# Decay and rate low-rank products in two row halves of the array, with their biases from fp32r products

## The reference

```
r, k, v, wd, ad, gd = split(h)                       # wd, ad: 64 wide
w_log = -softplus(-(w0 + tanh(wd) @ w_lora_up)) - 0.5
decay = exp(-exp(w_log))
a     = sigmoid(a0 + ad @ a_lora_up)                 # both 512 wide
```

## Time and profile before

| what | value |
|---|---|
| median of 3 runs | 2969.92 us (2968.96 to 2973.3) |
| the profiled execution | span 2963.8 us from the first to the last instruction, no other time is given for it; 6.1 us below the median |
| TensorE busy | 2899.2 us, 98% |
| VectorE, ScalarE, GpSimd busy | 54%, 34%, 50% |
| mixer | from about 597 to 1045 us of the span |

### The profile page before, as it was taken

One profiled execution on the slowest core, in us unless ns is written; L12 is line 12 of the kernel. 1 busy time (PEld: TensorE's weight loads), 2 busy tenths in 40 slices (PEclk: granted clock), 3 DMA queues, 4 the chain that ended last, 5 costly groups with the idle time before them and its releaser, 6 DMA issues. The chain is left out here.

```text
span 2963.8 us, 56296 instructions
## 1 busy us (share of the span) xinstructions
PE 2899.2 (98%) x23690; PEld 2474.9 (84%) x23690; DVE 1594.7 (54%) x2059; ACT 1000.5 (34%) x1740; POOL 1489.8 (50%) x1073
## 2 busy tenths in 40 slices
PE   8999999999999999999999999999999999999998
PEld 7888888888888879987888888887998788888887
DVE  7331634267777732329766654544233966664453
ACT  4122211245545432325333332232232533332222
POOL 4554544356666545266554533555427555543254
PEclk9999999989999999999999999999999999999999
DMA  4533455412223231112333356344111233336632
GB/s 160 183 114 96 126 167 183 146 50 61 65 57 80 71 100 43 43 50 76 115 119 140 128 192 223 142 175 156 42 46 49 85 114 135 138 111 238 230 142 85
DMA packets 175988, 346.65 MB, mean 117 GB/s; under 512 B 47233, under 2 KB 104705, under 8 KB 170113
## 3 DMA queue, kind: packets, MB, share of 16 engines
q1 hardware_dynamic: 175744, 343.16, 34.0%
HBM read 240.34 MB, written 102.76 MB: 116 GB/s over the span
## 5 line engine op out<-in xcount | busy, mean ns | idle before, releaser
L820 POOL TENSOR_TENSOR w_lo<-w_raw,w_hi 128x512 fp32r<-128x512 f32 x232 | 333.6, 1462 | 504.5 <-ACT w_hi L1124 501.0
L1679 PE MATMUL ps<-a_hi,w_hi 128*128 128x512 f32 x1140 | 445.3, 391 | 10.4 <-DVE a_lo L2396 10.0
L1679 PE MATMUL ps<-a_lo,w_hi 128*128 128x512 f32 x1140 | 444.3, 390 | 0.0
L1679 PE MATMUL ps<-a_hi,w_lo 128*128 128x512 f32 x1140 | 351.5, 390 | 0.0
L1124 ACT ACTIVATE w_hi<-w_raw 128x512 fp32r<-128x512 f32 x228 | 129.9, 623 | 625.5 <-PE ps L1679 474.7
L2216 PE MATMUL ps<-a_hi,w_hi 128*128 128x512 f32 x800 | 312.4, 391 | 11.5 <-ACT u_t L1499 4.9
L2216 PE MATMUL ps<-a_lo,w_hi 128*128 128x512 f32 x800 | 311.3, 389 | 0.0
L2216 PE MATMUL ps<-a_hi,w_lo 128*128 128x512 f32 x800 | 311.3, 389 | 0.0
L1679 PEld LDWEIGHTS ps<-a_hi,w_hi 128*128 128x128 f32 x1140 | 214.5, 188 | 55.0 <-DVE a_lo L2396 10.0
L1679 PEld LDWEIGHTS ps<-a_hi,w_lo 128*128 128x128 f32 x1140 | 214.3, 188 | 44.8
L1679 PEld LDWEIGHTS ps<-a_lo,w_hi 128*128 128x128 f32 x1140 | 214.5, 188 | 44.2 <-issue 0.2
(11 more groups left out here) (379 smaller groups left out, 6429.3 us busy)
## 6 DMA issues: line engine op xcount, KB each, us to landing
w_raw<-in_weights SPq DMA_DIRECT2D x228, 512.0 KB, 4.1
hidden<-hid SPq DMA_DIRECT2D x44, 1024.0 KB, 3.8
zT<-z_out SPq DMA_DIRECT2D x44, 512.0 KB, 3.3
a_hi<-hidden SPq DMA_DIRECT2D x44, 512.0 KB, 8.3
a_lo<-hidden SPq DMA_DIRECT2D x44, 512.0 KB, 9.4
w_raw<-kvw SPq DMA_DIRECT2D x32, 512.0 KB, 3.3
suv<-zT SPq DMA_DIRECT2D x16, 512.0 KB, 4.7
x<-in_xT SPq DMA_DIRECT2D x16, 512.0 KB, 6.0
```

The costliest lines, as they stand in the source:

```text
L820: pool.tensor_tensor(low_t[:, part, :], w_raw[:, u, part, :], high[:, part, :].bitcast(F32), ALU.subtract).then_inc(S["w_lo_done"], 1)
L1679: mm = pe.matmul(to[:, nb, 0:w], wt[:, k, :], r[:, k, nb * w:(nb + 1) * w], start=(k == 0 and r is hi_in and wt is high), stop=(k == kn - ...
```

## The change

The decay's and the rate's low-rank values come in one tile wad, decay in rows 0 to 63 and rate in rows 64 to 127, with two transfers in place of four. The weights lie in one tile wal in the same way. The products of the two halves alternate. The biases no longer have a row of ones. Two fp32r products of 32 rows each write them into the whole of bank 4 and bank 5 first: lora_b holds the biases by 128-channel block (a high and a remaining part in separate rows), ind is 1 where a row belongs to the block of 128 columns. VectorE prepares lora_b and ind in spatial().

```diff
-ZK_DMAS, ZV_DMAS = 10, 5
+ZK_DMAS, ZV_DMAS = 8, 5
...
-        wl = rw("wl", [P, RH * RN])
-        al = rw("al", [P, RH * RN])
+        wal = rw("wal", [P, RH * RN])
+        ind = rw("ind", [RN, HP * L], F32R)
+        lora_b = rw("lora_b", [RN, P], F32R)
...
-                for dst, src in ((wl, w_lora), (al, a_lora), (gl, g_lora), ...
+                for dst, src in ((wal, lora_up), (ind_in, lora_ind), (bias_in, lora_bias), (bias_sel, lora_sel), (gl, g_lora), ...
...
-                both_ways(wd[par][0:RN], zT[24], n, f"zk{par}")
-                both_ways(ad[par][0:RN], zT[25], n, f"zk{par}")
+                both_ways(wad[par], zT_t[12], n, f"zk{par}")
...
-            for t in (wd[0], ad[0], wd[1], ad[1]):
-                pool.memset(t[RN:P, :], 1.0).then_inc(S["rconst_done"], 1)
-            pool.wait_ge(S["rconst_done"], N_ONES)
...
-                act.activation(wd[par][0:RN, :], wd[par][0:RN, :], ACT.Tanh).then_inc(S["lora_in"], 1)
+                act.activation(wad[par][0:RN, :], wad[par][0:RN, :], ACT.Tanh).then_inc(S["lora_in"], 1)
...
-                low_rank(wl, wd[par], 4)
-                low_rank(al, ad[par], 5).then_inc(S["lwa_ps"], 1)
+                for e in range(2):
+                    rows = slice(32 * e, 32 * e + 32)
+                    pe.matmul(ps[:, 4 + e, :], lora_b[rows, :], ind[rows, :], start=True, stop=False, skip_group_check=True)
+                for m in range(HP):
+                    for e in range(2):
+                        mm = pe.matmul(cols(4 + e, m), wal[lane(e), m * P:(m + 1) * P], wad[par][lane(e), (m // 2) * C:(m // 2) * C + L],
+                                       start=False, stop=True, skip_group_check=True)
+                mm.then_inc(S["lwa_ps"], 1)
...
-                dve.wait_ge(S["rconst"], 16 * 19)
+                dve.wait_ge(S["rconst"], 16 * 21)
...
                 dve.wait_ge(S["const_ready"], 7)
+                dve.tensor_copy(ind[:], ind_in[:]).then_inc(S["rconst_done"], 1)
+                dve.tensor_copy(lora_b[:], bias_in[:]).then_inc(S["rconst_done"], 1)
+                dve.wait_ge(S["rconst_done"], 2)
+                dve.tensor_scalar(bias_in[:], bias_in[:], bias_sel[:, 0:1], None, ALU.mult).then_inc(S["rconst_done"], 1)
+                dve.wait_ge(S["rconst_done"], N_BIAS - 1)
+                dve.scalar_tensor_tensor(lora_b[:], lora_b[:].bitcast(F32), bias_sel[:, 1:2], bias_in[:], ALU.mult, ALU.add
+                                         ).then_inc(S["rconst_done"], 1)
+                dve.wait_ge(S["rconst_done"], N_BIAS)
                 dve.tensor_scalar(hc[:, 0, :], hc[:, 0, :], 0.5, None, ALU.mult).then_inc(S["const_ready"], 1)
```

More of the change, by code:

```diff
@@ L29 @@
 HP = RH // 2
-N_ONES, N_SET = 4, 6
+N_BIAS, N_SET = 4, 6
 L = 128
@@ L69, with hybrid_block_kernel @@
 G_IN, G_ATT, G_FF, G_FINAL, G_MEM = range(5)
[L72 removed]
+def hybrid_block_kernel(nc, xT, memT, gains, weights, shift_mu, lora_up, lora_bias, lora_sel, lora_ind, g_lora, head_cols,
                         kk_rows, lnx_rows, kk_cols, head_ones, w_spatialT, b_spatial, sgu_ln, consts, cen,
@@ L199, in hybrid_block_kernel @@
         wsr = place("wsr", [P, RH, L], F32, Z_END + 5 * KB)
-        wl = rw("wl", [P, RH * RN])
-        al = rw("al", [P, RH * RN])
+        ind_in = place("ind_in", [RN, HP * L], F32, Z_END + 9 * KB)
+        bias_in = place("bias_in", [RN, P], F32, Z_END + 15 * KB)
+        bias_sel = place("bias_sel", [RN, 2], F32, Z_END + 15 * KB + 512)
+        wal = rw("wal", [P, RH * RN])
+        ind = rw("ind", [RN, HP * L], F32R)
+        lora_b = rw("lora_b", [RN, P], F32R)
         gl = rw("gl", [P, RH * RN])
@@ L226, in hybrid_block_kernel @@
         suv = [rw(f"suv{i}", [P, 8, L]) for i in range(2)]
-        wd = [rw(f"wd{i}", [P, 3 * C]) for i in range(2)]
-        ad = [rw(f"ad{i}", [P, 3 * C]) for i in range(2)]
+        wad = [rw(f"wad{i}", [P, 3 * C]) for i in range(2)]
         gd = [rw(f"gd{i}", [P, 3 * C]) for i in range(2)]
@@ L548, in load_consts @@
                 sp.wait_ge(S["kvf_lo"], 2)
-                for dst, src in ((wl, w_lora), (al, a_lora), (gl, g_lora), (hc, head_cols), (kkr, kk_rows), (lnr, lnx_rows),
+                for dst, src in ((wal, lora_up), (ind_in, lora_ind), (bias_in, lora_bias), (bias_sel, lora_sel), (gl, g_lora), (hc, head_cols), (kkr, kk_rows), (lnr, lnx_rows),
                                  (heads, head_ones), (kkc, kk_cols), (hm, head_mean), (cent, cen), (id_in, half_ident), (tri_w, tri_wide),
@@ L3200 @@
     arrays["shift_mu"] = A(col(shift_mu[0]))
-    def padded(*parts):
-        parts = np.concatenate([np.asarray(r) for r in parts], 0)
-        out = np.zeros((P,) + parts.shape[1:], np.float32)
-        out[:parts.shape[0]] = parts
-        return out
-    arrays["w_lora"] = padded(w_lora_up[0], w0[0][None])
-    arrays["a_lora"] = padded(a_lora_up[0], a0[0][None])
+    arrays["lora_up"] = A(np.concatenate([np.asarray(w_lora_up[0]), np.asarray(a_lora_up[0])], 0))
+    bias = np.zeros((2, 32, P), np.float32)
+    sel = np.zeros((2, 32, 2), np.float32)
+    ind = np.zeros((2, 32, HP, L), np.float32)
+    for e, b in enumerate((w0, a0)):
+        for m in range(HP):
+            for r in (m, HP + m):
+                bias[e, r] = np.asarray(b[0]).reshape(HP, P)[m]
+                ind[e, r, m] = 1.0
+            sel[e, m] = 0.0, 1.0
+            sel[e, HP + m] = 1.0, -1.0
+    arrays["lora_bias"], arrays["lora_sel"], arrays["lora_ind"] = bias.reshape(RN, P), sel.reshape(RN, 2), ind.reshape(RN, HP * L)
     arrays["g_lora"] = A(np.asarray(g_lora_up[0]))
```

## The result

The changed kernel takes 2977.06 us (median of 20 runs, 2970.41 to 2982.95) against 2969.61 for the kernel before (20 runs, one of them stray at 14473): a ratio of 1.0026, 95% interval 1.0019 to 1.0032. It is slower by 7.5 us, where 2.8 faster was forecast, and outside the range. The two profiled executions differ by as much: spans of 2971.4 and 2963.8, so this pair of traces holds a loss of the same size.

What follows compares the result with a forecast made beforehand. TensorE, busy 98% of the span, was taken as the bound. The mixer's -5.6 us and the entry's +2.8 summed to -2.8, so 2969.9 became 2967.1 us, with a range of 2961 to 2973.

Steps and rivals of the forecast that it cites:

- rival 3: At the entry, the 4.75 us stall lowers TensorE's clock to half; short form 2968.8, long form 2978.1 at 0.08.
- the long form: At the entry, the 11.0 us job behind the stall runs at half clock: +11.0, total 2978.1 us; chance 0.08.
- the short form: At the entry, 3.4 us at half clock cost 1.7 us, total 2968.8; counted as upper part of the 0.42 forecast.
- The saving per group: In the mixer, decay and rate products fall from 1.88 to 1.53 us per group, saving 0.35; ends 0.00 and 0.55.
- the change of shape behind the keys' turn: In each mixer group, going from whole array to 32-row strips ahead of the bias products costs 0.10 us.
- beside each other, 0.23: In each mixer group, the two 32-row bias products run together in 0.23 us, not in turn at 0.46.
- Rival 2: In the mixer, array drains at each shape change and bias products run in turn: no saving, 2972.7 us; chance 0.13.
- The entry: Preparation in spatial(): TensorE starts its next job 4.75 us later, less 1.08, 0.45 and 0.4 given back: +2.8 us.
- Rival 1: At the entry, new VectorE instructions slip through together: 2963.6 us, chance 0.22; halfway, two of them free: 2965.2, chance 0.15.
- VectorE's turns with GpSimd: At the entry, four new VectorE instructions and hc each get in between two GpSimd instructions, hc done at 548.05.
- the two waits of 1.08 and 0.45: TensorE's waits before the first loras and on the suv transfer vanish, giving back 1.08 and 0.45 us.
- The saving in the mixer reaches the end: The group's later work shifts along, no new wait; 14 groups give 4.9 us and group 1 0.7, together 5.6.

Runs made afterwards that it cites:

- e1: Changed kernel with VectorE's four bias instructions moved two pairs earlier; 2974.79 us, +4.0 against the kernel before.
- e4: Kernel before plus only the new transfers and four VectorE bias instructions, result unused; 2975.91 us, +5.1 against the kernel before.
- e2: Changed kernel with group 1's 16 products as whole-array instructions; 2971.80 us, +1.0 against the kernel before.
- e3: Changed kernel with the bias instructions early and group 1's 16 products on the whole array; 2967.41 us, -3.4 against the kernel before.
- e7: e5 with bias products of 64 rows, 32 of them zeros; 2958.22 us, -11.3 against the kernel before.
- e13: Changed kernel with bias products of 64 rows, 32 of them zeros, preparation left in place; 2971.91 us, +2.1 against the kernel before.
- e9: e1 with group 1's 16 half-row products issued once more, ahead of the bias pair; 2967.02 us, ratio 0.9998 against the kernel before.
- e5: e1 with five redundant whole-array products filling TensorE's two longest pauses of body(-1); 2961.06 us, -8.5 against the kernel before, in two clumps.
- e8: e5 without the bias products, so the output lacks w0 and a0; 2951.56 us, -18.0 against the kernel before.
- e10: e1 with group 1's 16 half-row products reordered, eight of one half then eight of the other; 2974.95 us, +4.4 against the kernel before.

## Why the prediction was wrong

**The step that failed** is the clock in rival 3. It looked for the price of a low clock only where the change makes a new pause, at the entry, and gave the long form 0.08 there. At that place the dip was short (3.4 us at half, 1.7 lost), as the short form had it. The long half clock came at a place where the change makes no pause, where the clock was already at half, and where the products that the change replaces were the ones behind which it came back. The prediction read those rows for their length (group 1 saves 0.7) and not for the clock's return beside them. The sum had no term for it, and it cost 7.1 us net of the shorter products. That the cause is group 1's products and not the entry is shown by e1 (no entry pause, long half clock), e4 (entry pause, no long half clock) and e2 and e3 (whole-array products again, no long half clock, with and without the entry pause). That the time landed near the 2978.1 of the long form is luck: that form held the job behind the entry's pause at half clock for 11.0 us, which didn't happen.

**Terms that were mis-sized.**
- The saving per group: forecast 0.35, measured 0.27. The 16 products (1.10, measured 1.09) and the change of shape behind the keys' turn were right. The term that failed is the bias products "beside each other, 0.23" with 0.10 for the change behind: the pair takes 0.42 to 0.44 in all, with 64 rows it takes 0.23 (e7). The two do start beside each other, within 0.02 us; the time goes ahead of the next shape. Rival 2's full drain (no saving) did not occur.
- The entry: forecast +2.8 net of a stall of 4.75, measured +3.9. TensorE's pause was 4.04 us. The dip of the clock is 1.7 of the 3.9; without it the entry would be at 2.2. e1 minus after is -3.5 when each is taken against its own kernel before, so the runs agree. Rival 1, the quick entry, did not occur. Its sum is off by a little in itself: it finds 1.2 us for the five instructions and goes on with 1.3, and 1.3 - 1.08 - 0.45 - 0.4 is -0.6, not -0.7.

**Steps that were right.** VectorE's turns with GpSimd, one for one, with hc at 547.68 (forecast 547.9); no cover for the folded copy; the two waits of 1.08 and 0.45 at the first loras gone. The saving in the mixer reaches the end: from_values to from_values is 27.5 us on average after (639.49 to 969.60, twelve groups) and 27.75 before (628.21 to 961.21, twelve), 0.24 a group.

**What stays open.** It is shown that whole-array products for group 1 bring the clock back. Why 16 half-row products do so in some traces and not in others is open. A 32-row pair ahead of them is common to the four in which they did not, but the moment at which the stretch falls may count as well: e13's and e9's runs spread over both outcomes with the same instructions, and no experiment moved the moment alone. Only one run of each kernel has a trace. That the upper clumps of e5, e9 and e13 are lost clock is shown by the granted clocks of the runs; whether they lost it at the mixer's start or in a later dip (e3's profiled run has one of its own at 719 to 725) isn't seen. The 3.2 us by which e8 is faster than its saving of TensorE time are not traced to a place.

## What to carry to other kernels

Where a profile shows the clock at half, look at what stands at its return before replacing it: a block made shorter, with fewer rows in use, can cost more in clock than it saves in time, and the loss shows up far from any new wait. And look at the granted clock of every run, not only of the one with a trace: the same kernel can have both outcomes (e5, e9, e13). Products that use part of the array are worth giving the same rows as their neighbours, even if half of them are zeros (0.21 us a group here, e5 against e7). Before placing small VectorE work, see whether GpSimd runs beside it: four small instructions cost a 4 us stall of TensorE, and moved by some pairs they cost none (e1, where three of them last 0.21 to 0.34 us in place of 1.18 to 1.31).

## What was not expected of the hardware

TensorE at 34.00 of 34.00 us busy stayed at half clock (1.2 GHz of 2.4). The Trainium skill, TensorE: Matmul & The Clock Gate, Part 1, says that the throttled state is the default and activity releases it; here a TensorE that the profile shows busy throughout was not released, so the trace doesn't bear that sentence out, and the measurement decides. In e1 two whole-array blocks of 8 instructions, 2.07 us each (gd,gl and cent,zin, at 622.45 and 626.30), did not release it; sixteen in a row for group 1 did, in all five traces that have them.

Sixteen half-row products took 3.02 us at half clock when the eight of each half stood together (e10), and 2.00 when the halves alternated (e1): side by side they are faster by a third, not by half.

The three VectorE instructions of 64x128 elements lasted 1.2 to 1.3 us each beside GpSimd, and 0.21 to 0.34 in e1 where GpSimd was idle; the fp32r copy was held as much as the others. GpSimd's four lost 0.14 us together, and GpSimd was each time the first to start (543.59 against 543.84, 545.03 against 545.18). That is as the Trainium skill, SBUF — State Buffer, SBUF: two separate sides, has it, that the loser waits for the whole instruction; here the loser was the same engine each time.
